# A depthwise convolution shared out among four engines: two of its three TensorE chunks go to ScalarE products and GpSimd sums

## The reference, cut to what matters

```python
proj = x @ w_in[l]                                  # x: 256 tokens x 1024
q, k, v, a, g = jnp.split(proj, cuts, axis=-1)      # each 512 wide
attn = moba_attention(rope(q), rope(k), v)
conv = conformer_conv(a, g, conv_w[l], conv_b[l], conv_ln_g[l], conv_ln_b[l])
mixed = jnp.concatenate([attn, conv], axis=-1) @ w_out[l]
x = layer_norm(DEEPNORM_ALPHA * x + mixed, ...)
x = layer_norm(DEEPNORM_ALPHA * x + peer_ffn(x, ...), ...)

def conformer_conv(a, gate, w, b, g, beta):
    u = a * jax.nn.sigmoid(gate)
    u = causal_depthwise_conv(u, w) + b             # 31 taps, each channel by itself
    return jax.nn.silu(layer_norm(u, g, beta))      # norm over the 512 channels
```

## Time and profile before

| | |
|---|---|
| median of the runs | 1759.99 us (1759.82 to 1760.59) |
| the profiled execution: time | 1760.08 us |
| its span | 1757.9 us |
| its granted clock | 0.999 |
| busy: PE | 1745.2 us, 99% of the span |
| busy: DVE | 1473.0 us, 84% |
| busy: ACT | 1324.0 us, 75% |
| busy: POOL | 455.3 us, 26% |

### The profile page before, as it was taken

The page is one execution under the profiler, slowest core; times in us unless marked ns, Lnnn a source line. Parts: engine busy times, 40 slices in busy tenths (PEclk is TensorE's granted clock), DMA queues, the critical chain, the costliest instruction groups (busy, mean ns, idle before and its releaser), DMA issues.

```text
span 1757.9 us, 37807 instructions
## 1 busy us (share of the span) xinstructions
PE 1745.2 (99%) x14014; PEld 1370.5 (78%) x14014; DVE 1473.0 (84%) x2632; ACT 1324.0 (75%) x1773; POOL 455.3 (26%) x643
## 2 busy tenths in 40 slices
PE   9999999999999999999999999999999999999998
PEld 8789888899988888544487898888999888884443
DVE  8988989777878888788898799897877788877887
ACT  4689999888864445888746899998888644468885
POOL 0000011122223333555400100111222233335553
PEclk9999999999999999999999999999999999999999
DMA  8646565555545566666275556555555455757661
GB/s 261 205 159 212 194 203 191 192 191 179 187 132 172 180 240 226 228 203 204 86 215 190 183 193 203 201 191 195 184 179 181 135 177 169 262 202 239 204 203 37
DMA packets 96005, 333.52 MB, mean 190 GB/s; under 512 B 11680, under 2 KB 16032, under 8 KB 95648
## 3 DMA queue, kind: packets, MB, share of 16 engines
q1 hardware_dynamic: 88992, 317.51, 53.5%
q10 hardware_dynamic: 6912, 14.77, 2.7%
HBM read 328.20 MB, written 4.03 MB: 189 GB/s over the span
## 4 chain that ended last, share of the span: by engine, by line
PE 96%; ACT 2%; DVE 1%; issue 0%; POOL 0%; DVEq 0%; POOLq 0%; ACTq 0%
PE bank L1889 15%; PE bank L1891 15%; PE bank L1890 15%; PE bank L1956 9%; PE bank L1958 8%; PE bank L1957 8%; PE bank L1972 6%; PE bank L1976 6%; PE bank L1974 6%; PE bank L2239 3%; PE bank L2046 1%; PE bank L2197 1%; ACT probs L869 0%; PE bank L1911 0%; PE bank L1918 0%; PE bank L1941 0%
## 5 line engine op out<-in xcount | busy, mean ns | idle before, releaser
L1891 PE MATMUL bank<-xt_half,half_tiles 128*128 128x256 f16 x2272 | 619.2, 273 | 0.0
L1890 PE MATMUL bank<-xt_half,half_tiles 128*128 128x256 f16 x2272 | 619.1, 273 | 0.0
L1889 PE MATMUL bank<-xt_half,half_tiles 128*128 128x256 f16 x2272 | 619.0, 272 | 0.0
L1185 DVE SCALAR_TENSOR_TENSOR half_tiles<-raw,to_half,half_tiles 128x1024 f16<-128x1024 f32 x280 | 357.8, 1278 | 79.9 <-ACT half_tiles L724 78.4
L714 ACT ACTIVATE hi<-raw 128x1024 fp32r<-128x1024 f32 x184 | 194.7, 1060 | 234.8 <-PE bank L1958 194.4
L724 ACT ACTIVATE half_tiles<-raw,to_half 128x1024 f16<-128x1024 f32 x280 | 319.5, 1141 | 3.7 <-POOL to_half L606 3.4
L606 POOL TENSOR_SCALAR to_half<-unit_bound 128x1 int32<-128x1 int32 x144 | 59.4, 412 | 855.3 <-DVE unit_bound L1176 855.3
L732 ACT ACTIVATE squares_unread<-raw 128x2048 bf16<-128x2048 f32 x140 | 266.3, 1902 | 0.0
L1168 DVE TENSOR_TENSOR lo<-raw,hi 128x1024 fp32r<-128x1024 f32 x184 | 240.1, 1309 | 4.4 <-ACT hi L714 3.1
L1891 PEld LDWEIGHTS bank<-xt_half,half_tiles 128*128 128x128 f16 x2272 | 221.6, 98 | 26.5
L1889 PEld LDWEIGHTS bank<-xt_half,half_tiles 128*128 128x128 f16 x2272 | 221.7, 98 | 26.0
(11 more groups left out here) (259 smaller groups left out, 2761.7 us busy)
## 6 DMA issues: line engine op xcount, KB each, us to landing
raw<-in_stream SPq DMA_DIRECT2D x464, 512.0 KB, 3.7
v_raw<-in_stream SPq DMA_DIRECT2D x128, 512.0 KB, 4.1
early_raw<-in_stream SPq DMA_DIRECT2D x8, 512.0 KB, 4.9
shifted_u<-x_kept ACTq DMA_DIRECT2D x16, 142.0 KB, 5.1
ln_g<-in_ln_p ACTq DMA_DIRECT2D x4, 512.0 KB, 6.7
ln_b<-in_ln_p ACTq DMA_DIRECT2D x4, 512.0 KB, 8.7
keys_sb<-in_keys_t ACTq DMA_DIRECT2D x2, 1024.0 KB, 6.1
x_kept<-x ACTq DMA_DIRECT2D x4, 512.0 KB, 3.6
```

What stands on the lines that cost most here:

```text
L1185: vec.scalar_tensor_tensor(here[:, 1, :], raw_of(f), to_half[:, slot:slot + 1], here[:, 0, :], ALU.mult, ALU.subtract)\
L1889: mm(dst, weight(0, slot, k), xt[:, k, 0, :], start=k == 0, stop=False)
L1890: mm(dst, weight(0, slot, k), xt[:, k, 1, :], start=False, stop=False)
L1891: last = mm(dst, weight(1, slot, k), xt[:, k, 0, :], start=False, stop=k == KC - 1)
```

## The change

The strips keep only chunk 3. Chunk 1 is wholly made as products: ScalarE multiplies a window of `u_pad` by one tap (L877 of the changed kernel) into one of 8 slots, and GpSimd adds the slot to a running sum (L657). Chunks 0 and 2 are shared: VectorE does taps 1 to 24 of chunk 0 and taps 1 to 25 of chunk 2 on `acc`, 49 in all; ScalarE begins their sums with tap 0 and the bias; the last 6 and 5 taps are ScalarE products that GpSimd sums in `xc`, which VectorE adds to `acc` at the end (`add_part`). GpSimd adds 39 products in a layer: 5 for chunk 0, 30 for chunk 1 and 4 for chunk 2. GpSimd also clears the margins of `u_pad` and makes the one spread table that is left. `acc_done` now also waits for the last of GpSimd's sums. The same happens in both layers.

```diff
-TAP_STEPS = (2, 8, 8)
+TAP_STEPS = (8,)
...
-DVE_TAPS = ((0, 0, 4, 3, 4, 4, 4, 3), (4, 4, 4, 4, 2, 6, 4, 4))
+PARTS_OF_TAPS = {0: (1, 25), 2: (1, 26)}
+DVE_TAPS = ((0, 0, 4, 3, 4, 4, 4, 3), (4, 3, 3, 4, 3, 4, 4, 2))
+POOL_TAPS = {0: (25, TAPS), 1: (0, TAPS), 2: (26, TAPS)}
+ADDED = (0,) * 5 + (1,) * 6 + (1, 2) * 4 + (1,) * 20
+ACT_TAPS = ((0, 0, 2, 3, 3, 3, 3, 3), (4, 4, 4, 4, 3, 3, 0, 0))
+PRODUCTS = 8
...
+                if layer:
+                    pool.wait_ge(*tile_used(layer - 1, TILES))
+                nc.gpsimd.memset(u_pad[:, :, 0:TAPS - 1], 0.0).then_inc(*pads_made.one)
...
+                for n in range(SHIFTED):
+                    spread_taps(n)
...
+                for n, c in enumerate(ADDED):
+                    total = (xc, acc, xc)[c][:, c, :]
+                    if c in last_added:
+                        pool.wait_ge(*tap_added(layer, last_added[c] + 1))
+                    else:
+                        pool.wait_ge(*tap_begun(layer, (2, 3, 5)[c]))
+                    pool.wait_ge(*product_made(layer, n + 1))
+                    nc.gpsimd.tensor_tensor(total, total, products[:, n % PRODUCTS, :], ALU.add)\
+                      .then_inc(*tap_added.one)
+                    last_added[c] = n
...
+                def tap_products(count):
+                    for i in range(multiplied[0], multiplied[0] + count):
+                        c, n = ADDED[i], ADDED_TAP[i]
+                        if i >= PRODUCTS:
+                            act.wait_ge(*tap_added(layer, i - PRODUCTS + 1))
+                        nc.scalar.activation(products[:, i % PRODUCTS, :], u_pad[:, c, n:n + SEQ],
+                                             ACT.Copy, scale=conv_sb[:, c, n:n + 1])\
+                          .then_inc(*product_made.one)
...
+                    if n == AG0 + 2:
+                        act.wait_ge(*conv_in(layer, 1))
+                        act.wait_ge(*pads_made(layer, 2))
+                        act.wait_ge(*conv_u(layer, 1))
+                        begin_sum(acc, 0, 0)
+                        begin_part(xc, 0, POOL_TAPS[0][0])
...
+                    tap_products(ACT_TAPS[0][n - AG0])
...
                     def taps(count, chunks):
...
-                        if n == (0, PE_SHARE)[c]:
-                            tap_step[c] = step(vec.tensor_scalar(
-                                acc[:, c, :], window, weight, conv_sb[:, c, TAPS:TAPS + 1],
-                                ALU.mult, ALU.add))
+                        if c in tap_step:
+                            step.settle(tap_step[c])
                         else:
-                            step.settle(tap_step[c])
-                            tap_step[c] = step(vec.scalar_tensor_tensor(
-                                acc[:, c, :], window, weight, acc[:, c, :], ALU.mult, ALU.add))
+                            dve.wait_ge(*tap_begun(layer, (1, 3, 4)[c]))
+                        tap_step[c] = step(vec.scalar_tensor_tensor(
+                            acc[:, c, :], window, weight, acc[:, c, :], ALU.mult, ALU.add))
...
+                def add_part(c):
+                    dve.wait_ge(*tap_added(layer, len(ADDED) - ADDED[::-1].index(c)))
+                    step.settle(tap_step[c])
+                    tap_step[c] = step(vec.tensor_tensor(acc[:, c, :], acc[:, c, :], xc[:, c, :],
+                                                         ALU.add))
...
-                    if m == 1:
-                        spread_taps()
...
                     if c < CT - 1:
-                        taps(count, max(1, min(m // 2, 2)))
+                        taps(count, (0,))
...
                 for m, count in enumerate(DVE_TAPS[1]):
                     rest(0, QKV0 + m + LO_LEAD)
-                    taps(count, 2)
+                    taps(count, (0, 2))
+                    if m == KC - 2:
+                        add_part(0)
+                        add_part(2)
...
-                dve.wait_ge(*conv_ps(layer, 1))
-                step(vec.tensor_tensor(acc[:, 1, :], conv_banks[1][:, 0:SEQ], acc[:, 1, :],
-                                       ALU.add))
+                dve.wait_ge(*tap_added(layer, len(ADDED)))
                 step.settle()
                 dve.sem_inc(*acc_done.one)
...
-                pe.wait_ge(*conv_out(layer, 2))
+                pe.wait_ge(*conv_out(layer, 1))
                 pe.wait_ge(*acc_done(layer, 1))
                 sums_of_chunks(0, acc)
```

More of the change, by code:

```diff
@@ L87 @@
 TOTALS = CW // STRIP
-DVE_TAPS = ((0, 0, 4, 3, 4, 4, 4, 3), (4, 4, 4, 4, 2, 6, 4, 4))
-assert sum(map(sum, DVE_TAPS)) == 2 * TAPS - PE_SHARE
+TAP_COLUMNS = 3 * PER_CHUNK - SHIFTS
+PARTS_OF_TAPS = {0: (1, 25), 2: (1, 26)}
+DVE_TAPS = ((0, 0, 4, 3, 4, 4, 4, 3), (4, 3, 3, 4, 3, 4, 4, 2))
+assert sum(map(sum, DVE_TAPS)) == sum(end - first for first, end in PARTS_OF_TAPS.values())
+POOL_TAPS = {0: (25, TAPS), 1: (0, TAPS), 2: (26, TAPS)}
+ADDED = (0,) * 5 + (1,) * 6 + (1, 2) * 4 + (1,) * 20
+ADDED_TAP = [POOL_TAPS[c][0] + 1 + ADDED[:n].count(c) for n, c in enumerate(ADDED)]
+assert all(ADDED.count(c) == end - first - 1 for c, (first, end) in POOL_TAPS.items())
+ACT_TAPS = ((0, 0, 2, 3, 3, 3, 3, 3), (4, 4, 4, 4, 3, 3, 0, 0))
+assert sum(map(sum, ACT_TAPS)) == len(ADDED)
+PRODUCTS = 8
 PROBS_RING = 4
@@ L124 @@
 assert (WIDE + 1) * (NARROW + 1) > TOPK
-DVE_STEPS = 431
+DVE_STEPS = 424
 class Signal:
@@ L271, in build @@
         k_t = inside("k_t", 63488, [P, PAIRS, SEQ])
-        four_taps = inside("four_taps_of_strips", 68608, [P, SHIFTS, SHIFTED * PER_CHUNK - SHIFTS])
+        four_taps = inside("four_taps_of_strips", 68608, [P, SHIFTS, TAP_COLUMNS])
         tri_f = inside("causal_f", 67584, [P, P])
@@ L276, in build @@
         shifted = [inside(f"shifted_u{n}", at, [P, SHIFTS, WINDOW])
-                   for n, at in enumerate((73728, 86016, 90624))]
+                   for n, at in enumerate((86016,))]
         spread = [inside(f"spread_taps{n}", at, [P, SHIFTS, TAP_STEPS[n], STRIP])
-                  for n, at in enumerate((79872, 95232, 99328))]
+                  for n, at in enumerate((99328,))]
+        products = inside("tap_products", 90624, [P, PRODUCTS, SEQ])
         mixed = inside("mixed", 104320, [P, KC, 2, SEQ], f32r)
@@ L608, in unit_to_half, with spread_taps @@
                                             ALU.mult, ALU.add).then_inc(*unit_made.one)
+                def spread_taps(n):
+                    first = (STRIP_CHUNKS[n] - 1) * PER_CHUNK
+                    taps_of = slice(first, first + SHIFTS * (TAP_STEPS[n] - 1) + 1, SHIFTS)
+                    shape = [P, SHIFTS, TAP_STEPS[n], STRIP]
+                    nc.gpsimd.tensor_tensor(
+                        spread[n][:, :, :, :],
+                        four_taps[:, :, taps_of][:, :, :, None].to_broadcast(shape),
+                        strip_sum[:, None, None, :].to_broadcast(shape), ALU.mult)\
+                      .then_inc(*spread_made.one)
+                if layer:
+                    pool.wait_ge(*tile_used(layer - 1, TILES))
+                nc.gpsimd.memset(u_pad[:, :, 0:TAPS - 1], 0.0).then_inc(*pads_made.one)
+                nc.gpsimd.memset(u_pad[:, :, TAPS - 1 + SEQ:WINDOW], 0.0).then_inc(*pads_made.one)
+                pool.wait_ge(*four_taps_in(layer, SHIFTS))
+                pool.wait_ge(*pads_made(layer, 2))
+                past = slice(PER_CHUNK + TAPS - SHIFTS + 1, TAP_COLUMNS, PER_CHUNK)
+                nc.gpsimd.memset(four_taps[(SHIFTS - 1) * STRIP:, :, past], 0.0)\
+                  .then_inc(*past_cleared.one)
+                pool.wait_ge(*past_cleared(layer, 1))
+                pool.wait_ge(*strips_summed(0, SHIFTS - 1))
+                for n in range(SHIFTED):
+                    spread_taps(n)
+                last_added = {}
+                for n, c in enumerate(ADDED):
[8 more added lines that the diff above has]
+                    last_added[c] = n
                 unit_to_half(0)
@@ L790, in keep_u @@
                 def keep_u(n):
-                    act.wait_ge(*conv_u(layer, CT - SHIFTED + n + 1))
-                    act.dma_start(kept_columns(n), u_pad[:, CT - SHIFTED + n, :])\
+                    c = STRIP_CHUNKS[n]
+                    act.wait_ge(*conv_u(layer, c + 1))
+                    act.dma_start(kept_columns(n), u_pad[:, c, :])\
                        .then_inc(*u_kept[n].one)
@@ L803, in load_shifted, with begin_sum, begin_part @@
                            .then_inc(*shifted_in[n].one)
+                def begin_sum(dst, c, n):
+                    nc.scalar.activation(dst[:, c, :], u_pad[:, c, n:n + SEQ], ACT.Identity,
+                                         scale=conv_sb[:, c, n:n + 1],
+                                         bias=conv_sb[:, c, TAPS:TAPS + 1])\
+                      .then_inc(*tap_begun.one)
+                def begin_part(dst, c, n):
+                    nc.scalar.activation(dst[:, c, :], u_pad[:, c, n:n + SEQ], ACT.Copy,
```

(13 more changed lines are left out.)

37 lines of the change are left out of this document (20 added, 17 removed).

## The result

The changed kernel takes 1795.49 us, the median of four runs (1794.48 to 1795.83), against 1760.23 us for the kernel before in its runs beside them. The ratio is 1.0198, with a 95% interval of 1.0185 to 1.0211: slower by 35 us. The forecast was 1796, and slower.

A forecast was written before the change was run, and what follows sets the result against it. TensorE was taken to bound the kernel, VectorE deciding after 1 us of relative growth. Layers cost 18.3 and 18.7 us, 37 in all, 36 kept: 1760.08 becomes 1796, range 1779 to 1808 (8 in 10: 1776 to 1812).

The forecast's parts named there:

- TensorE's 4.43 us a layer: Strips on TensorE: 10 of 18 steps go, at 0.443 us each, 8.9 us in both layers.
- VectorE's own list, +0.3 us: VectorE's sums from the first `u_pad`: fewer taps, more chaining and two `xc` additions make them 0.3 us longer a layer.
- the spread tables bring nothing: Ahead of VectorE's first `u_pad`: removing 2.69 us of tables only opens idle time before the sigmoid's end, gain 0.
- The collision, 18.3 us a layer: 39 GpSimd additions a layer each push back a VectorE tap or `rest` by 0.55 us, less free time: 18.3 us.
- the 2-port modes alone: Rival of no collision: taps beside GpSimd's additions go free, VectorE ends at 62.7, 1759 us; chance 0.05.
- GpSimd keeps up: GpSimd's additions stay about three entries ahead of VectorE, hiding the added `acc_done` wait; rival of GpSimd last: 1808, chance 0.06.
- ScalarE costs nothing: ScalarE's 44 added instructions, some 19 us a layer, fit into 28 us free in the stage: 0.
- The norm behind it, +0.6 us a layer: Behind L2072: VectorE's `rest` and rotation end 0.6 us after TensorE's L2079, delaying the sum that waits for them.
- 0.4 for the smaller cover: Second layer, before the first sum over channels: less cover than the first layer's 1.06 us, so 18.7 instead of 18.3.
- The clock: Rival: waiting drops TensorE to 1.2 GHz, a tile takes 5.6 instead of 4.4 us, 14 us a layer, 1824; chance 0.06.
- the taps were to take 0.95 us: Sign in the profile after: VectorE's taps in the stage near 0.95 us instead of 0.42.
- TensorE was to wait some 18 us a layer for `lo`: Sign in the profile after: TensorE idle before the QKV tiles, released by `lo`, some 18 us in each layer's stage.

The follow-up runs named there:

- the run with one column: The changed kernel with GpSimd's 39 additions of a layer cut from 128 x 256 to 128 x 1, sums incomplete: 1759.86 us, ratio 0.9999.
- the rebalanced runs: Changed kernel with running sums of chunks 0 and 2 in PSUM, and 16 or 24 taps of chunk 2 on the strips: 1758.91 and 1760.58 us.
- the idle additions: The kernel before with only 39 GpSimd additions of 128 x 256 a layer added, on a spare buffer: 1794.41 us, ratio 1.0194.

## Why the prediction was right

**TensorE's 4.43 us a layer.** Right: the strips take 4.32 less, and where nothing else is late 8.4 us come out in the two layers together.

**VectorE's own list, +0.3 us.** Right: +0.5. That the spread tables bring nothing is right too: VectorE stands idle for 3.40 us ahead of the first `u_pad`, where they used to be.

**The collision, 18.3 us a layer.** Right, and the decisive term. VectorE's sums take 80.93 - 18.04 = 62.9 us from the first `u_pad`, 45.2 without the additions: 17.7. The way to it was partly luck in the pieces. I counted 0.55 us for each of 39 and took 3.2 off for free time; the runs show 0.46 for each on average, the free part included. And the forecast end of VectorE's sums, 81.0 against 80.93, is closer than its terms: the first `u_pad` came 0.35 us later than before (18.04, 17.69), where I had taken it as fixed, the list was 0.2 longer and the collision 0.6 shorter. The rule with two SBUF inputs, of the Trainium skill's "GPSIMD Engine Reference", section Specifications, holds in this case, by the run with sums in PSUM. The note of the Trainium skill's "Advanced Engine Details and Errata", section Mode Summary, names the 2-port modes alone; taken as the whole rule it would have given the 1759 of the run with one column, and the trace does not agree with that.

**GpSimd keeps up.** Right: its last addition ends at 67.11, 14 us ahead of VectorE's sums. But ScalarE did wait for a free slot, 1.3 us in the first layer, where I had expected none; VectorE's pace hid it.

**ScalarE costs nothing.** Right: with products of one column, half of their time gone, the ratio stays within the noise.

**The norm behind it, +0.6 us a layer, and 0.4 for the smaller cover.** Wrong, and small. From the first sum over channels to the first scores behind it TensorE took 75.01 - 63.45 = 11.56 us before and 92.75 - 81.12 = 11.63 after: +0.1, not +0.6. The second layer adds 17.70 to the first one's 17.67, so the 0.4 doesn't show either. I had 37 from the terms and kept 36; the spans differ by 35.5.

**The clock.** I gave a fall of TensorE's clock 0.06 and a price of 28 us. It did fall, to a granted 0.83 and 0.66 in stretches of 10 us, so the condition of the rival came true and its price did not: L2139 starts 0.2 us after VectorE's end (80.93, 81.12), and the profile has no wait of VectorE between 19 and 81 us, so the slower products ran inside time in which TensorE would have waited. The step that failed there is "4.4 us becomes 5.6 for each tile": the clock was low only in parts of the stage.

**Of the signs** named ahead, the taps were to take 0.95 us; they take 0.75 on average, because 39 additions meet 64 taps and rests, and the last 10 taps run alone. TensorE was to wait some 18 us a layer for `lo`; the profile has 10.3 for `lo` and 5.1 for `q_rotated`.

## What to carry to other kernels

An idle engine is not free if it works on the same memory as a full one. Before elementwise work moves to GpSimd, count the VectorE instructions beside it that have two SBUF operands, and charge VectorE with each GpSimd instruction. Here an addition cost VectorE 0.46 us, as much as a tap that it would have done itself (0.40 to 0.48), so nothing was unloaded from it. Look at one-input instructions from SBUF to SBUF too: the one seen here paid as well. If the running sum of the VectorE instruction can lie in PSUM, the charge goes away, as it did for 49 taps a layer here. And look at everything that the slowed engine feeds: in the rebalanced runs TensorE waited for late rests in the first half of the stage, and that took the gain although VectorE's sums were ready.

## What the runs showed of the hardware that I had not expected

- An addition on GpSimd of 128 columns costs VectorE 0.17 us and one of 256 columns 0.46: less than half for half the length (runs with 128 columns and with 256, each against one column).
- A VectorE tap with its running sum in PSUM is as fast as in SBUF: 484 against 480 ns, chained ones included.
- A one-input VectorE instruction from SBUF to SBUF (L1357 beside the idle additions) was pushed back as well, from 0.41 to 0.83 us.
- TensorE's granted clock was 0.66 in a stretch where it was busy 4.89 of 10 us, with one wait of 5.1, and 0.83 in one where it was busy 7.37, while in the first 10 us of the execution it stood at 1.00 at 5.83 busy.
